# Moving two parts of an S5 operand construction from VectorE to GpSimd

## Chip, cores and metric

The kernel runs on all 8 cores of one Trainium2 chip. Every core has the same program on its own 4096 tokens. The metric is the device time of the slowest core in microseconds.

## What is computed

The reference is one layer of a hybrid encoder: a combined input projection, a gated MLP branch (A), an S5 state space branch (B), a gated merge, and a SwiGLU block. The change touches only constants of branch B. Each of 32 groups has 16 channels and 64 complex states; with the step dt, the recurrence and its readout are

```
mag = exp(lam_re * dt); ab = mag * (cos(lam_im * dt) + i sin(lam_im * dt))
bb  = ((ab - 1) / lam) * b
x_t = ab * x_(t-1) + bb @ u_t
y_t = Re(c @ x_t) + d * u_t
```

The kernel does not scan token by token. It works on blocks of 8 tokens x 16 channels = 128 rows, with matrices made once per group from powers of ab: R_all takes the inputs of a block to its contribution to the state, T_all is the response inside a block, O_all takes the state to the outputs of a block, and D_all (three per group) multiplies the state, real and imaginary parts stacked on 128 partitions, by ab to the 8th, 16th and 24th.

## The kernel before

Each core runs a generation of these matrices, a first main part (eight supertiles of 1024 tokens: norm, projection, block states, a scan over blocks; then the S5 outputs), and a second main part (eight tiles of 512 tokens: the gated MLP, the merge, SwiGLU). The program order of each engine is the order of the calls in the source. A small scheduler in the source holds tokens: `run` makes the engine wait for the tokens of all writers of what is read or written; a `Buf` keeps the tokens of its last writers in `w`.

The generation is `emit_s5_gen`, called once at L302. Its inputs are small loads by SP. Nearly all its arithmetic is on VectorE, with [128, 32] and [128, 32, 16] float32 tiles, through the helper `dv`, which writes the single Buf `G`. So each instruction waits for the one before it, and `G.w` is one token after each `dv`.

- L1089 to L1091 (`wz`) make one slice of 512 columns of a product of complex powers and coefficients, three instructions each. They are called 32 times: 8 positions s, for MR, MRm, Om (float32) and O_all (bf16).
- The group loop makes R_all and T_all for 32 groups: TensorE transposes MR (L1101), ScalarE copies it out (L1103), TensorE multiplies MRm and Om (L1106), VectorE masks the result (L1108) and adds the skip term (L1110). Writers of `G` are kept with `acc=True`, so a group's steps follow each other across the engines.
- Two `cmul` (L1069 to L1074) make the 16th and 24th power. L1119 to L1123 make D_all: for each of 3 powers and 32 groups one tensor_scalar and one fused scalar_tensor_tensor of 128 columns.
- 37 small VectorE instructions (L1004 to L1009, L1129 to L1135) make AA and BB for the scan.

After the generation there is `barrier(skip_pq=True)`: all engines and the SP queue wait for the last token of all engines. Behind it are the load of the projection weights (L324, SP) and the load of the first supertile of x_prev (L336). The latter is issued from the GpSimd queue, as are the conversions of the weights to bf16 in DRAM, of which a first part (L216) is issued ahead of the generation and the rest behind the first x_prev load.

Of the kernel before, what the change touches and what calls it, by code (L numbers as in the profile page):

```python
# [7 lines left out]
F32 = mybir.dt.float32  # L8
BF16 = mybir.dt.bfloat16
AF = mybir.ActivationFunctionType  # L10
ALU = mybir.AluOpType
# [58 lines left out]
def run(E, fns, reads=(), writes=(), acc=False, nowait=False):  # L70
    if not isinstance(fns, (list, tuple)):
        fns = [fns]
    for b in reads:
        for t in b.w:
            E.wait(t)
    for b in writes:
        if nowait:
            continue
        for t in b.w:
            E.wait(t)  # L80
        for t in b.r:
            E.wait(t)
    for f in fns[:-1]:
        E.emit_nosig(f)
    tok = E.emit(fns[-1])
    for b in reads:
        b.r.append(tok)
        if len(b.r) > 64:
            b.r = b.r[-64:]
    for b in writes:  # L90
        if acc:
            b.w.append(tok)
        else:
            b.w = [tok]
            b.r = []
    return tok


def build_program():
# [177 lines left out]
    if S5_ON:  # L277
# [22 lines left out]
        run(SQ, lambda e: e.dma_start(out=S_f, in_=c_swap_f[:, :]), writes=[B_const], acc=True)  # L300
        run(SQ, lambda e: e.dma_start(out=S_bf, in_=c_swap_bf[:, :]), writes=[B_const], acc=True)
        G_gen = emit_s5_gen(run, Buf, dict(PE=PE, ACT=ACT, DVE=DVE, POOL=POOL, SQ=SQ), Alloc(gen_base), dram,  # L302
                            psf, PSF, ident_f, B_const,
                            dict(R_all=R_all, T_all=T_all, O_all=O_all, AA=AA, BB=BB, D_all=D_all, S_f=S_f))
# [609 lines left out]
def emit_s5_gen(run, Buf, E, AL, dram, psf, PSF, ident_f, B_const, outs):  # L914
    PE, ACT, DVE, POOL, SQ = E["PE"], E["ACT"], E["DVE"], E["POOL"], E["SQ"]
    G = Buf()
# [5 lines left out]
    def dv(fn):  # L922
        run(DVE, fn, writes=[G])
# [29 lines left out]
    for i_, dst_ in enumerate((lr2, li2, dcol)):  # L953
        run(PE, lambda e, i_=i_: e.transpose(out=psf[:, 1, 0:32], in_=stg[0:32, i_, :], identity=ident_f[0:32, 0:32]),
            reads=[G, B_const], writes=[PSF[1]])
# [5 lines left out]
    for (cst, C2) in ((cst_re, Cre2), (cst_im, Cim2)):  # L961
        for r in range(4):
            run(PE, lambda e, cst=cst, r=r: e.transpose(out=psf[:, 0, 0:128], in_=cst[:, r, :], identity=ident_f),
                reads=[G, B_const], writes=[PSF[0]])
            run(DVE, lambda e, C2=C2, r=r: e.tensor_copy(out=C2[:, r * 8:(r + 1) * 8, :],
                                                         in_=psf[:, 0, 0:128].rearrange("p (a h) -> p a h", h=16)),
                reads=[PSF[0]], writes=[G])

    def t32():
        return AL.get([32], F32)  # L970
# [63 lines left out]
    Z1 = AL.get([32, 16], F32)  # L1034
    Z2 = AL.get([32, 16], F32)

    def bc16(a):
        return a.unsqueeze(2).to_broadcast([128, 32, 16])
# [7 lines left out]
    lo, hi = slice(0, 64), slice(64, 128)  # L1046
# [8 lines left out]
    Pr = AL.get([16, 32], F32)  # L1055
    Pi_ = AL.get([16, 32], F32)
# [11 lines left out]
    def cmul(orr, oii, xr, xi, yr, yi):  # L1068
        dv(lambda e: e.tensor_tensor(out=t1, in0=xr, in1=yr, op=ALU.mult))  # L1069
        dv(lambda e: e.tensor_tensor(out=t2, in0=xi, in1=yi, op=ALU.mult))  # L1070
        dv(lambda e: e.tensor_tensor(out=orr, in0=t1, in1=t2, op=ALU.subtract))
        dv(lambda e: e.tensor_tensor(out=t1, in0=xr, in1=yi, op=ALU.mult))
        dv(lambda e: e.tensor_tensor(out=t2, in0=xi, in1=yr, op=ALU.mult))
        dv(lambda e: e.tensor_tensor(out=oii, in0=t1, in1=t2, op=ALU.add))  # L1074
# [8 lines left out]
    Om = AL.get([32, 128], F32)  # L1083
    O_all = outs["O_all"]
    tm = AL.get([32, 16], F32)
    tmT = AL.get([128], F32)

    def wz(dst, kidx, A1, A2):
        dv(lambda e: e.tensor_tensor(out=tm, in0=A1, in1=bc16(Pr[:, kidx, :]), op=ALU.mult))  # L1089
        dv(lambda e: e.tensor_tensor(out=dst, in0=A2, in1=bc16(Pi_[:, kidx, :]), op=ALU.mult))  # L1090
        dv(lambda e: e.tensor_tensor(out=dst, in0=dst, in1=tm, op=ALU.add))  # L1091

    for s in range(8):
        wz(MR[:, :, 16 * s:16 * s + 16], 7 + (7 - s), X1, X2)
        wz(MRm[:, :, 16 * s:16 * s + 16], 7 - s, X1, X2)
        wz(Om[:, :, 16 * s:16 * s + 16], 7 + s, Z1, Z2)
        wz(O_all[:, :, 16 * s:16 * s + 16], 7 + s + 1, Z1, Z2)
    R_all, T_all = outs["R_all"], outs["T_all"]
    for g in range(32):
        pb = g % 2  # L1100
        run(PE, lambda e, g=g, pb=pb: e.transpose(out=psf[:, pb, 0:128], in_=MR[:, g, :], identity=ident_f),  # L1101
            reads=[G, B_const], writes=[PSF[pb]])
        run(ACT, lambda e, g=g, pb=pb: e.activation(out=R_all[:, g, :], in_=psf[:, pb, 0:128], func=AF.Copy),  # L1103
            reads=[PSF[pb]], writes=[G], acc=True)
        pt = 2 + g % 2
        run(PE, lambda e, g=g, pt=pt: e.matmul(psf[:, pt, 0:128], MRm[:, g, :], Om[:, g, :], start=True, stop=True),  # L1106
            reads=[G], writes=[PSF[pt]])
        run(DVE, lambda e, g=g, pt=pt: e.tensor_tensor(out=tmT, in0=psf[:, pt, 0:128], in1=maskT, op=ALU.mult),  # L1108
            reads=[PSF[pt], G], writes=[GT_])
        run(DVE, lambda e, g=g: e.scalar_tensor_tensor(out=T_all[:, g, :], in0=ident_f, scalar=dcol[:, g:g + 1], in1=tmT,  # L1110
                                                        op0=ALU.mult, op1=ALU.add),
            reads=[GT_, G, B_const], writes=[G], acc=True)
    D_all, S_f = outs["D_all"], outs["S_f"]
    p16r, p16i, p24r, p24i, c2 = (t32() for _ in range(5))
    cmul(p16r, p16i, Pr[:, 15, :], Pi_[:, 15, :], Pr[:, 15, :], Pi_[:, 15, :])
    cmul(p24r, p24i, p16r, p16i, Pr[:, 15, :], Pi_[:, 15, :])
    tmD = AL.get([128], F32)
    for k, (br_, bi_) in enumerate(((Pr[:, 15, :], Pi_[:, 15, :]), (p16r, p16i), (p24r, p24i))):
        dv(lambda e, bi_=bi_: e.tensor_copy(out=c2[lo], in_=bi_[lo]))  # L1119
        dv(lambda e, bi_=bi_: e.tensor_scalar(out=c2[hi], in0=bi_[hi], scalar1=-1.0, scalar2=None, op0=ALU.mult))  # L1120
        for g in range(32):
            dv(lambda e, g=g: e.tensor_scalar(out=tmD, in0=S_f, scalar1=c2[:, g:g + 1], scalar2=None, op0=ALU.mult))
            dv(lambda e, g=g, k=k, br_=br_: e.scalar_tensor_tensor(out=D_all[:, k, g, :], in0=ident_f, scalar=br_[:, g:g + 1],  # L1123
                                                                    in1=tmD, op0=ALU.mult, op1=ALU.add))
    AA, BB = outs["AA"], outs["BB"]
    for _ in range(5):
        sq_u()
# [5 lines left out]
    dv(lambda e: e.tensor_copy(out=BB[hi, 0:32], in_=A8i[hi]))  # L1133
    dv(lambda e: e.tensor_copy(out=BB[lo, 32:64], in_=A8i[lo]))
    dv(lambda e: e.tensor_scalar(out=BB[hi, 32:64], in0=A8i[hi], scalar1=-1.0, scalar2=None, op0=ALU.mult))  # L1135
    return G


# [46 lines left out]
```

How the kernel before makes its waits and increments, by code:

```python
            def f(eng):  # L889
                for o in E.ops:
                    if o[0] == "w":
                        eng.wait_ge(sems[o[1]], o[2])
                    else:
                        ins = o[1](eng)
                        if o[2] is not None:
                            ins.then_inc(sems[o[2]], o[3])
```

## Time and profile before

| | |
|---|---|
| three runs | 3766.16, 3760.68, 3764.14 us; median 3764.14 us |
| profiled execution | 3765.08 us |
| span of its cores 0 to 7 | 3763.2, 3752.1, 3748.6, 3752.4, 3762.4, 3749.3, 3743.6, 3750.0 us |
| mean granted TensorE clock by core | 0.830 to 0.833 |
| generation (core 0) | from 0 to 440.92 us |

All rows are from core 0, the slowest one. Times are microseconds from the start of the span unless marked ns. "L1122" is the line of the kernel. A group's row gives its total busy time and the mean of one instruction, then the idle time ahead of them on their engine. An arrow names what ended a wait. PE is TensorE, PEld its weight load, DVE VectorE, ACT ScalarE, POOL GpSimd.

### The profile page before, as it was taken

The numbers are of one execution on the slowest core, as the hardware profiler recorded it, in microseconds if no ns is written. First come the engines' busy times: TensorE is split into PE (matmuls) and PEld (weight loads), VectorE is DVE, ScalarE is ACT, GpSimd is POOL, SyncE is SP. The second block draws the span as 40 slices with busy tenths as digits, with TensorE's granted clock in tenths as the row PEclk, the third lists the DMA queues.
The fourth block names the chain that finished last, engine by engine and source line by source line (L and its number), as shares of the span: only waits on it lengthen the run. The fifth ranks groups of instructions, "written<-read, shape, count | busy, mean of one in ns | idle before, by whom it ended". The sixth has DMA issues, their size and how long they took to land.

```text
span 3763.2 us, 43146 instructions; the slowest of 8 cores (3743.6 to 3763.2 us)
## 1 busy us (share of the span) xinstructions
PE 2346.3 (62%) x13686; PEld 1187.1 (32%) x13686; DVE 1249.0 (33%) x3251; ACT 1185.0 (31%) x1714; POOL 89.5 (2%) x168
## 2 busy tenths in 40 slices
PE   0012046666544377957957868777795795796875
PEld 0001024445432133423423423333342342342332
DVE  0753523565633223224213313312322321331321
ACT  0000146655545342242332322323224233232221
POOL 0000001010000000000000000000000000000000
PEclk9999966666666588978978988888897897898988
DMA  2000295897000423423424243243342242433422
GB/s 26 0 0 0 42 109 79 101 124 75 1 7 1 129 79 95 157 89 101 133 97 146 94 137 123 87 143 102 112 143 98 90 146 84 145 99 108 130 87 69
DMA packets 274338, 337.69 MB, mean 90 GB/s; under 512 B 40836, under 2 KB 249640, under 8 KB 273096
## 3 DMA queue, kind: packets, MB, share of 16 engines
q1 hardware_dynamic: 231592, 251.99, 21.4%
q0 software_dynamic: 42528, 82.95, 13.4%
q8 instruction: 118, 1.93, 0.2%
q14 instruction: 100, 0.82, 0.1%
HBM read 367.41 MB, written 49.28 MB: 111 GB/s over the span
## 4 chain that ended last, share of the span: by engine, by line
PE 52%; DVE 17%; ACT 16%; issue 9%; DMA 5%; DVEq 1%; another core or an unknown queue 1%; ACTq 0%; POOLq 0%; POOL 0%; SPq 0%
PE psf L845 8%; PE psf L851 8%; PE psf L860 8%; PE psf L766 5%; PE psf L793 3%; PE psf L812 3%; PE psf L361 3%; PE psf L754 3%; ACT arena L502 2%; DMA out<-arena 2%; DVE arena L671 2%; ACT arena L343 2%; PE psf L799 2%; PE psf L399 1%; PE psf L448 1%
## 5 line engine op out<-in xcount | busy, mean ns | idle before, releaser
L845 PE MATMUL psf<-arena 128*128 128x512 bf16 x1408 | 346.2, 391 | 12.7 <-DVE arena L649 12.7
L851 PE MATMUL psf<-arena 128*128 128x512 bf16 x1408 | 337.3, 383 | 0.0
L860 PE MATMUL psf<-arena 128*128 128x512 bf16 x1408 | 305.2, 379 | 10.1 <-DVE arena L854 10.1
L766 PE MATMUL psf<-arena 128*128 128x512 bf16 x1024 | 254.0, 410 | 83.9 <-ACT arena L769 83.9
L754 PE MATMUL psf<-arena 128*128 128x512 bf16 x512 | 153.7, 468 | 234.0 <-ACT arena L758 234.0
L854 DVE TENSOR_TENSOR arena<-arena,psf 128x512 bf16<-128x512 f32 x176 | 120.8, 687 | 382.9 <-PE psf L851 346.4
L671 DVE TENSOR_TENSOR arena<-arena,psb 128x1024 f32<-128x1024 f32 x64 | 75.9, 1217 | 472.6 <-PE psb L667 472.6
L351 PE MATMUL psb<-arena 128*128 128x128 bf16 x512 | 57.7, 293 | 249.5 <-DMA arena<-x_prev 156.3
L849 ACT ACTIVATE arena<-psf 128x512 f32<-128x512 f32 x176 | 104.2, 597 | 321.2 <-PE psf L845 319.1
L845 PEld LDWEIGHTS psf<-arena 128*128 128x128 bf16 x1408 | 138.5, 100 | 179.9 <-issue 27.9
L851 PEld LDWEIGHTS psf<-arena 128*128 128x128 bf16 x1408 | 139.4, 99 | 172.0 <-issue 10.1
L860 PEld LDWEIGHTS psf<-arena 128*128 128x128 bf16 x1408 | 137.1, 98 | 178.2 <-issue 13.8
L766 PEld LDWEIGHTS psf<-arena 128*128 128x128 bf16 x1024 | 105.0, 104 | 226.8 <-issue 127.3
L793 PE MATMUL psf<-arena 128*128 128x512 bf16 x512 | 134.1, 410 | 45.7 <-DVE arena L746 45.7
L754 PEld LDWEIGHTS psf<-arena 128*128 128x128 bf16 x512 | 58.0, 115 | 327.1 <-issue 292.3
L815 ACT ACTIVATE arena<-psf 128x512 bf16<-128x512 f32 x64 | 38.2, 597 | 319.0 <-PE psf L812 319.0
L1101 PE MATMUL psf<-arena 128*128 128x128 f32 x32 | 14.3, 446 | 193.6 <-DVE arena L1091 154.4
L632 ACT ACTIVATE arena<-arena 128x1024 bf16<-128x1024 f32 x64 | 67.6, 1056 | 208.5 <-DVE arena L631 171.6
L742 DVE TENSOR_TENSOR arena<-arena 128x1024 f32<-128x1024 bf16 x32 | 39.2, 1226 | 278.9 <-ACT arena L736 278.9
L863 ACT ACTIVATE arena<-psf 128x512 bf16<-128x512 f32 x64 | 38.2, 597 | 290.0 <-PE psf L860 290.0
L351 PEld LDWEIGHTS psb<-arena 128*128 128x128 bf16 x512 | 47.1, 133 | 259.0 <-issue 256.7
L812 PE MATMUL psf<-arena 128*128 128x512 bf16 x512 | 115.2, 387 | 15.8 <-DVE arena L805 15.8
(227 smaller groups left out, 3406.8 us busy)
## 6 DMA issues: line engine op xcount, KB each, us to landing
arena<-win_d SPq DMA_DIRECT2D x65, 1024.0 KB, 5.4
arena<-wfd_d SPq DMA_DIRECT2D x64, 704.0 KB, 4.6
arena<-wfg_d SPq DMA_DIRECT2D x40, 1024.0 KB, 5.7
arena<-wfu_d SPq DMA_DIRECT2D x40, 1024.0 KB, 7.8
arena<-x_own POOLq DMA_DIRECT2D x32, 512.0 KB, 6.9
arena<-wa_d SPq DMA_DIRECT2D x16, 1024.0 KB, 10.2
arena<-wo_d SPq DMA_DIRECT2D x16, 1024.0 KB, 6.0
out<-arena POOLq DMA_DIRECT2D x32, 512.0 KB, 2.9
```

The source lines that it names most:

```text
L351: run(PE, [lambda e, k=k, s_=s_, pb=pb, xb_=xb_: e.transpose(out=psb[:, pb, k * 128:(k + 1) * 128], in_=xcm[:, xb_, s_, k * 128:(k + 1) * ...
L361: run(PE, [lambda e, k=k, s_=s_, pb=pb: e.matmul(psf[:, pb, :], hTs[:, k, s_, :], wBg[:, k, :], start=(k == 0), stop=(k == 7)) for k in ra ...
L671: run(DVE, lambda e, b=b, pb=pb, xs=xs: e.tensor_tensor(out=xb2[:, xs, b, :], in0=xb2[:, xs, b, :], in1=psb[:, pb, :], op=ALU.add), reads= ...
L754: run(PE, [lambda e, k=k, gg=gg, pb=pb, wu=wu: e.matmul(psf[:, pb, :], wu[:, k, gg * 128:(gg + 1) * 128], hTa[:, k, :], start=(k == 0), st ...
L766: run(PE, [lambda e, k=k, mm=mm, pb=pb, wg=wg: e.matmul(psf[:, pb, :], wg[:, k, mm * 128:(mm + 1) * 128], hTa[:, k, :], start=(k == 0), st ...
L793: run(PE, [lambda e, k=k, mm=mm, p3=p3, wa_=wa_: e.matmul(psf[:, p3, :], wa_[:, k, mm * 128:(mm + 1) * 128], ya[:, k, :], start=(k == 0), ...
L812: run(PE, [lambda e, k=k, mm=mm, pb=pb, wo_=wo_: e.matmul(psf[:, pb, :], wo_[:, k, mm * 128:(mm + 1) * 128], mg[:, k, :], start=(k == 0), ...
L845: run(PE, [lambda e, k=k, ff=ff, p1=p1, wg_=wg_: e.matmul(psf[:, p1, :], wg_[:, k, ff * 128:(ff + 1) * 128], hTb[:, k, :], start=(k == 0), ...
L849: run(ACT, lambda e, p1=p1, sa=sa: e.activation(out=scr[:, sa, :], in_=psf[:, p1, :], func=AF.Silu), reads=[PSF[p1]], writes=[SCR[sa]])
L851: run(PE, [lambda e, k=k, ff=ff, p2=p2, wu_=wu_: e.matmul(psf[:, p2, :], wu_[:, k, ff * 128:(ff + 1) * 128], hTb[:, k, :], start=(k == 0), ...
L854: run(DVE, lambda e, f=f, p2=p2, sa=sa: e.tensor_tensor(out=act[:, f, :], in0=scr[:, sa, :], in1=psf[:, p2, :], op=ALU.mult), reads=[SCR[s ...
L860: run(PE, [lambda e, f=f, pb=pb, wd_=wd_: e.matmul(psf[:, pb, :], wd_[:, f, :], act[:, f, :], start=(f == 0), stop=(f == NF - 1)) for f in ...
```

## The change

`wz` gets a second form on GpSimd, through a helper `pl` with its own Buf `GP` and its own temporary. Om and O_all use it, in a loop of their own behind the loop for MR and MRm. The product of MRm and Om then also waits for `GP`. D_all goes to GpSimd too; its fused instruction becomes two, since a second tensor_scalar and a tensor_tensor take the place of the scalar_tensor_tensor. The pairs of copies into `c2` are made for all three powers ahead of the D_all loop, into three tiles. At the end the tokens of `GP` are added to those of `G`.

```diff
+    GP = Buf()
+    tmP = AL.get([32, 16], F32)
+
+    def pl(fn):
+        for t_ in G.w:
+            POOL.wait(t_)
+        run(POOL, fn, writes=[GP])
+
+    def wz(dst, kidx, A1, A2, on_pool=False):
+        ex, tt_ = (pl, tmP) if on_pool else (dv, tm)
+        ex(lambda e: e.tensor_tensor(out=tt_, in0=A1, in1=bc16(Pr[:, kidx, :]), op=ALU.mult))
+        ex(lambda e: e.tensor_tensor(out=dst, in0=A2, in1=bc16(Pi_[:, kidx, :]), op=ALU.mult))
+        ex(lambda e: e.tensor_tensor(out=dst, in0=dst, in1=tt_, op=ALU.add))
 
     for s in range(8):
         wz(MR[:, :, 16 * s:16 * s + 16], 7 + (7 - s), X1, X2)
         wz(MRm[:, :, 16 * s:16 * s + 16], 7 - s, X1, X2)
-        wz(Om[:, :, 16 * s:16 * s + 16], 7 + s, Z1, Z2)
-        wz(O_all[:, :, 16 * s:16 * s + 16], 7 + s + 1, Z1, Z2)
+    for s in range(8):
+        wz(Om[:, :, 16 * s:16 * s + 16], 7 + s, Z1, Z2, on_pool=True)
+        wz(O_all[:, :, 16 * s:16 * s + 16], 7 + s + 1, Z1, Z2, on_pool=True)
...
         run(PE, lambda e, g=g, pt=pt: e.matmul(psf[:, pt, 0:128], MRm[:, g, :], Om[:, g, :], start=True, stop=True),
-            reads=[G], writes=[PSF[pt]])
+            reads=[G, GP], writes=[PSF[pt]])
...
-    for k, (br_, bi_) in enumerate(((Pr[:, 15, :], Pi_[:, 15, :]), (p16r, p16i), (p24r, p24i))):
-        dv(lambda e, bi_=bi_: e.tensor_copy(out=c2[lo], in_=bi_[lo]))
-        dv(lambda e, bi_=bi_: e.tensor_scalar(out=c2[hi], in0=bi_[hi], scalar1=-1.0, scalar2=None, op0=ALU.mult))
+    tmD2 = AL.get([128], F32)
+    c2k = [t32() for _ in range(3)]
+    pows = ((Pr[:, 15, :], Pi_[:, 15, :]), (p16r, p16i), (p24r, p24i))
+    for k, (br_, bi_) in enumerate(pows):
+        dv(lambda e, bi_=bi_, k=k: e.tensor_copy(out=c2k[k][lo], in_=bi_[lo]))
+        dv(lambda e, bi_=bi_, k=k: e.tensor_scalar(out=c2k[k][hi], in0=bi_[hi], scalar1=-1.0, scalar2=None, op0=ALU.mult))
+    for k, (br_, bi_) in enumerate(pows):
         for g in range(32):
-            dv(lambda e, g=g: e.tensor_scalar(out=tmD, in0=S_f, scalar1=c2[:, g:g + 1], scalar2=None, op0=ALU.mult))
-            dv(lambda e, g=g, k=k, br_=br_: e.scalar_tensor_tensor(out=D_all[:, k, g, :], in0=ident_f, scalar=br_[:, g:g + 1],
-                                                                    in1=tmD, op0=ALU.mult, op1=ALU.add))
+            pl(lambda e, g=g, k=k: e.tensor_scalar(out=tmD, in0=S_f, scalar1=c2k[k][:, g:g + 1], scalar2=None, op0=ALU.mult))
+            pl(lambda e, g=g, br_=br_: e.tensor_scalar(out=tmD2, in0=ident_f, scalar1=br_[:, g:g + 1], scalar2=None, op0=ALU.mult))
+            pl(lambda e, g=g, k=k: e.tensor_tensor(out=D_all[:, k, g, :], in0=tmD, in1=tmD2, op=ALU.add))
...
+    G.w = list(G.w) + list(GP.w)
     return G
```

## Rows read from the trace of the kernel before

**Rows 1.** The page: busy time by engine; the span in 40 slices.
```profile
PE 2346.3 (62%) x13686; PEld 1187.1 (32%) x13686; DVE 1249.0 (33%) x3251; ACT 1185.0 (31%) x1714; POOL 89.5 (2%) x168
PE   0012046666544377957957868777795795796875
DVE  0753523565633223224213313312322321331321
ACT  0000146655545342242332322323224233232221
DMA  2000295897000423423424243243342242433422
```

**Rows 2.** Windows: stretch, its length, busy us and instructions by engine, clock, DMA.
```profile
160.90:238.10 77.20, 0.00 (x0) 0.00 (x0) 66.45 (x96) 0.00 (x0) 0.00 (x0) 1.00 0.00 0
238.10:341.90 103.80, 38.82 (x96) 21.86 (x96) 20.55 (x64) 10.15 (x33) 0.00 (x0) 1.00 0.00 0
341.90:346.30 4.40, 0.00 (x0) 0.00 (x0) 2.66 (x14) 0.00 (x0) 0.00 (x0) 1.00 0.01 2
346.30:430.15 83.85, 0.00 (x0) 0.00 (x0) 61.96 (x196) 0.00 (x0) 0.00 (x0) 1.00 0.00 0
430.15:441.00 10.85, 0.00 (x0) 0.00 (x0) 6.96 (x37) 0.00 (x0) 0.00 (x0) 1.00 0.00 0
```

**Rows 3.** The chain that ended last, behind the barrier.
```profile
442.93 22.18 DMA arena<-x_prev
465.25 1.16 ACT arena L343 x2
```

**Rows 4.** Groups of VectorE, the first of the `wz` lines; all three alike.
```profile
L1089 DVE TENSOR_TENSOR arena<-arena 128x512 f32<-128x512 f32 x32 | 22.2, 692 | 3.7 <-DVE arena L1091 0.5
```

**Rows 5.** Timeline: first and last `wz` instruction, first instructions of the group loop.
```profile
160.98 0.69 DVE L1089 TENSOR_TENSOR arena<-arena 128x512 f32<-128x512 f32 x1
...
237.31 0.69 DVE L1091 TENSOR_TENSOR arena<-arena 128x512 bf16<-128x512 bf16 x1
...
238.25 0.45 PE L1101 MATMUL psf<-arena 128*128 128x128 f32 x1 [154.44 <-DVE arena L1091]
238.84 1.28 ACT L1103 ACT_TABLE_LOAD   x1 [238.84 <-PE psf L1101]
...
240.56 0.77 PE L1106 MATMUL psf<-arena 128*128 128x128 f32 x2 [1.86 <-ACT arena L1103]
```

**Rows 6.** Timeline: end of the group loop, `cmul`, start of D_all.
```profile
341.48 0.35 DVE L1110 SCALAR_TENSOR_TENSOR arena<-arena 128x128 bf16<-128x128 f32 x1
341.93 0.19 DVE L1069 TENSOR_TENSOR arena<-arena 128x32 f32<-128x32 f32 x1
...
345.84 0.17 DVE L1119 COPY arena<-arena 64x32 f32<-64x32 f32 x1
346.12 0.18 DVE L1120 TENSOR_SCALAR arena<-arena 64x32 f32<-64x32 f32 x1
346.40 0.28 DVE L1122 TENSOR_SCALAR arena<-arena 128x128 f32<-128x128 f32 x1
```

**Rows 7.** Groups of VectorE from 341.9 to 442.
```profile
L1123 DVE SCALAR_TENSOR_TENSOR arena<-arena 128x128 bf16<-128x128 f32 x96 | 33.8, 352 | 11.1 <-DVE arena L1122 1.4
L1122 DVE TENSOR_SCALAR arena<-arena 128x128 f32<-128x128 f32 x96 | 27.5, 286 | 10.3
```

**Rows 8.** Timeline: last instruction of the generation, first DMA behind the barrier.
```profile
440.74 0.18 DVE L1135 TENSOR_SCALAR arena<-arena 64x32 f32<-64x32 f32 x1
...
442.93 0.55 POOL L336 DMA_DIRECT2D arena<-x_prev  x1 [368.50 <-issue]
```

**Rows 9.** GpSimd: timeline of two dependent memsets; two groups of the whole span.
```profile
74.11 0.10 POOL L958 MEMSET arena<- 128x1 f32 x1 [54.53 <-DMA arena<-c_mask_toep]
74.33 0.10 POOL L959 MEMSET arena<- 128x1 f32 x1
...
L677 POOL DMA_DIRECT2D arena<-x_own x32 | 16.9, 530 | 1.5 <-issue 0.3
L589 POOL MEMSET arena<- 128x128 bf16 x1 | 0.2, 204 | 398.8 <-DVE arena L587 398.8
```

More of the change, by code:

```diff
@@ L1086, in emit_s5_gen @@
     tmT = AL.get([128], F32)
[L1088 to L1091, printed above, removed]
+    GP = Buf()
[9 more added lines that the diff above has]
+        ex(lambda e: e.tensor_tensor(out=dst, in0=dst, in1=tt_, op=ALU.add))
     for s in range(8):
@@ L1113, in emit_s5_gen @@
     D_all, S_f = outs["D_all"], outs["S_f"]
-    p16r, p16i, p24r, p24i, c2 = (t32() for _ in range(5))
+    p16r, p16i, p24r, p24i = (t32() for _ in range(4))
     cmul(p16r, p16i, Pr[:, 15, :], Pi_[:, 15, :], Pr[:, 15, :], Pi_[:, 15, :])
```

## The prediction

> **What bounds the kernel now.** I read the page first, for where the changed code sits, then the windows by stage, then the timeline at each seam, then the groups of the two engines concerned. The page shows [rows 1]: TensorE is the busiest engine at 62% of the span, VectorE has 33%, GpSimd 2%. Taken as averages they say that VectorE is not the bound and that GpSimd has room. The slices say something else about the changed code: it lies in the first 441 us, where TensorE and ScalarE are nearly idle, the DMA share is 0 after the first 60 us, and VectorE is the only busy engine. The windows cut that stretch up [rows 2]: the four products MR, MRm, Om and O_all (96 VectorE instructions in 77 us, nothing else running), the loop over 32 groups (T_all and R_all, TensorE 38.8 us, VectorE 20.6 us and ScalarE 10.2 us of 103.8 us, one after another), 4.4 us of powers, the D_all loop (196 instructions in 83.9 us, again VectorE alone), and 37 small instructions in 10.9 us. Then comes the barrier, and behind it the first load of x_prev starts the main work: the chain of waits goes from the end of this stretch into that DMA and from it into ScalarE [rows 3]. So every microsecond by which the last operand is finished later or earlier moves all 3320 us behind it by the same amount. Nothing in this prologue is covered by anything else. That the engine shares call GpSimd free is beside the point; what counts is whether GpSimd works at the same time as VectorE, and how long its chain is.
>
> **Can the two engines overlap?** The new helper copies G.w at the time of the call, and each call on VectorE has replaced G.w by its own last token. The Om and O_all calls are written after all MR and MRm calls, so the first GpSimd product waits for the last MRm add. The D_all calls are written after the group loop, after the two cmul and after the six c2k copies, so they wait for the last of these. While GpSimd makes Om and O_all, VectorE has nothing: its next instruction is the mask multiply of group 0 (L1108), which needs TensorE's MRm x Om product, and that now waits for GP, the last token of all 48 GpSimd instructions, O_all's included. TensorE runs in order, so behind that wait are queued the transposes of groups 1 to 31; ScalarE waits for those, VectorE for the products. Only the transpose of group 0 and ScalarE's table load get ahead. The one real overlap is D_all on GpSimd beside the last 37 VectorE instructions.
>
> **The change part by part**, on the profiled execution's time base:
>
> 1. MR and MRm stay on VectorE. The four products run from 160.98 to 238.00 [rows 4, 5]: 77.0 us for 96 instructions, 0.80 us each (692 ns busy and a gap of 0.1 us). Half of them end at 161.0 + 38.5 = 199.5.
> 2. Om and O_all: 48 GpSimd instructions of 512 columns, at p each from start to start. A wait across engines costs 0.25 us, as from the last add to TensorE's transpose (238.00 to 238.25) [rows 5]. They run from 199.75 to 199.75 + 48p.
> 3. The group loop, from TensorE's first MRm x Om at 240.56 to the end of the last L1110 at 341.83, is 101.3 us [rows 5, 6]. The table load of 1.28 us that stood ahead of that matmul is now hidden under item 2. End of loop: 199.75 + 0.25 + 48p + 101.3 = 301.3 + 48p.
> 4. Twelve cmul instructions (341.93 to 345.84, 3.9 us) and now all six c2k halves at 0.28 us (1.7 us) instead of two [rows 6]: 5.6 us, and 0.25 us to reach GpSimd. D_all starts at 307.1 + 48p.
> 5. D_all: VectorE needed 96 pairs of 286 and 352 ns [rows 7]. GpSimd needs 96 triples (two tensor_scalar and one tensor_tensor of 128 columns, because the fused operation is split), t each, and every one waits for the one before, since all write GP. End: 307.1 + 48p + 96t.
> 6. The 37 small VectorE instructions (10.9 us) leave the path; they end at about 307 + 11 + 48p, under item 5. If GpSimd were so fast as to finish inside them they would set the end again.
> 7. Now the end is at 440.92 [rows 8], and from there to the x_prev issue it is 2.0 us, which stays: the same waits, on the same GpSimd queue, ahead of the same DMA. No DMA is moved past anything; the 10 early conversions on that queue have been issued long before, and the later ones stand behind the barrier before and after. SP's queue waits at the same barrier.
>
> So the change is 48p + 96t - 133.8 us. The break-even is 133.8 us of GpSimd work in 336 instructions, 0.40 us each.
>
> **What is p, what is t?** The trace has no GpSimd arithmetic at all, only memsets and DMA issues [rows 9]. Two dependent memsets of one column start 0.22 us apart; a memset of 128 columns takes 204 ns against 98 ns, so a column costs 0.835 ns in one pass that only writes. Bounds from these rows:
> - Below: every instruction costs one pass, whatever it reads. p = 0.22 + 0.43 = 0.65, t = 3 x 0.327 = 0.98; 31 + 94 = 125 us, a gain of 8.5 us. An instruction can't be cheaper than a memset of its size.
> - Inputs are read one after the other and the write is hidden behind: p = 0.22 + 0.855 = 1.075, t = 0.327 + 0.327 + 0.434 = 1.09; 52 + 104 = 156 us, a loss of 22 us.
> - Every operand, read or written, costs its pass: p = 0.22 + 1.28 = 1.50, t = 0.434 + 0.434 + 0.541 = 1.41; 72.1 + 135.2 = 207 us, a loss of 73.5 us.
> - Above: the fixed part is not a memset's 0.22 us but that of the other GpSimd instruction of the trace, a DMA issue with 0.53 us. That adds 0.31 x 336 = 104 us: a loss of 178 us.
> I take the third. The memset is the nearest row for the fixed part, but it reads nothing, and the new instructions also fetch a pointer scalar, a broadcast operand or a strided output; so I count all passes instead of hiding one. It would make an Om instruction (about 1.4 us busy) twice as long as VectorE's 692 ns. The weight of a fixed part above 0.22 us is on the high side of the range: each 0.1 us there is 34 us.
>
> The Trainium skill, "GPSIMD Engine Reference", section "Performance versus the Vector engine", speaks against the change: a two-input elementwise instruction costs about 2.6 cycles of 1.2 GHz per element there, one with a single input about line rate, and VectorE is roughly twice as fast. No row here shows GpSimd arithmetic to hold that against. Worked out from the page as an estimate, p = 1.33 and t = 1.15, together 174 us, a loss of 40 us instead of 73.5.
>
> **Sum**: 207.3 - 133.8 = +73.5 us. The profiled execution took 3765.1 us (span 3763.2 us), 0.9 us above the median of 3764.1. On the median: 3837.6 us, 2.0% slower.
>
> **Rivals.**
> - *Passes overlap.* Cheaper reads, 22 to 45 us of loss, 3786 to 3809 us. For it: a streaming engine need not serialize its write. Against it: only a write-only row gives the slope. 0.17.
> - *Fixed cost dominates.* 288 of the 336 instructions have only 128 columns, so if dispatch plus the wait for one's own predecessor is 0.35 to 0.53 us, the loss is 117 to 178 us, 3881 to 3942 us. For it: the DMA issues at 0.53 us each. Against it: the two dependent memsets at 0.22 us. 0.18.
> - *The other side: one pass for every operation.* If GpSimd takes p = 0.65 and t = 0.98, the end comes at 432 and the kernel takes about 3756 us, 0.2% faster, because the 10.9 us of small VectorE instructions and the table load are hidden. It decides where 336 GpSimd instructions average under 0.40 us. For it only the write-only slope; against it, no row shows this engine reading a tensor at that rate. 0.04.
> - *Contention.* The 37 VectorE instructions beside D_all could hold GpSimd up, at most by their own busy time, 7 us; 3845 us. The change as written would be hurt little, because it overlaps so little. 0.03.
> - *The split loop does not do what it says.* If Om really ran beside MR, 38.5 us would be saved and the loss would be 35 us. The token list excludes it: G.w holds the last MRm add when the first GpSimd product is written. 0.00.
>
> The rule on contention is in the Trainium skill, "SBUF — State Buffer", section "SBUF: two separate sides": VectorE with two SBUF inputs and a GpSimd instruction that reads SBUF hold a shared port pair exclusively, one fully blocking the other. By it the contention rival is real, for some 7 us.
>
> TensorE's clock stays out of the sum. The granted clock is 1.00 (2.4 GHz) over the whole stretch [rows 2], though TensorE had been idle for 154 us before the group loop; a longer wait ahead of it should leave it there.
>
> **How the numbers follow.** My forecast has 0.58: 3815 to 3860 us, p and t within some 10% of the third case. With the others: the range from 3790 to 3915 us takes in the upper half of the overlapping case and the dispatch case up to a fixed part of 0.45 us; some 0.07 is left out below it and 0.08 above. What this kernel's measurement can tell from no change is some 0.2% (7.5 us), so faster 0.03, same 0.03, slower 0.94.
>
> **What the changed profile would show.** VectorE empty from about 199.5 until the first L1108; 48 GpSimd instructions there with 1.5 us from start to start; TensorE's first MRm x Om at about 272; a group loop of the same 101 us; D_all on GpSimd from about 379 to 514, with triples of 1.4 us; VectorE done at about 390 and idle after; the x_prev issue at about 516 instead of 442.93. Everything after it the same, shifted. The prediction is wrong if triples take under 1.0 or over 2.0 us, or if the main part, from the x_prev issue to the end, changes its length.

## The result and the profile after

The changed kernel takes 3901.12 us (median of 9 runs) against 3765.76 us for the kernel before (median of 10 runs): a ratio of 1.0357, 95% interval 1.0344 to 1.0369, so 3.6% and some 135 us slower. Executions in which one die of the chip was disturbed occur with every kernel here; the ratios leave them out, and where too few others are left below, the profiled execution is given instead.

The page of the kernel after (its slowest core is core 7) answers to [rows 1]:

```profile
PE 2348.0 (60%) x13686; PEld 1188.7 (31%) x13686; DVE 1155.1 (30%) x3011; ACT 1185.0 (30%) x1714; POOL 302.2 (8%) x504
DVE  1712001456563322322322312322321331331321
POOL 0051770101000000000000000000000000000000
```

VectorE has lost 94 us of work and GpSimd has gained 213 us. A slice is 97 us long here, and only in the third and the fourth do both have a digit. The windows by stage show that even there they hardly work at the same time; the columns are those of [rows 2], the busy time of PE, PEld, DVE, ACT and POOL in this order, then the clock and the DMA:

```profile
160.00:198.86 38.86, 0.00 (x0) 0.00 (x0) 33.42 (x49) 0.00 (x0) 0.00 (x0) 1.00 0.00 0
198.86:259.00 60.14, 0.48 (x2) 0.25 (x2) 0.00 (x0) 1.56 (x2) 53.08 (x48) 1.00 0.00 0
259.00:360.50 101.50, 38.34 (x95) 21.60 (x95) 20.34 (x64) 8.59 (x31) 0.00 (x0) 1.00 0.00 0
360.50:366.50 6.00, 0.00 (x0) 0.00 (x0) 3.92 (x21) 0.00 (x0) 0.00 (x0) 1.00 0.00 0
366.50:575.50 209.00, 0.00 (x0) 0.00 (x0) 7.28 (x36) 0.00 (x0) 159.39 (x288) 1.00 0.00 0
```

The first two rows are the first row of [rows 2] torn in two: VectorE for 39 us, then GpSimd for 60 us with VectorE at zero. The group loop takes what it took before, 101.5 us (before, 101.3 us from TensorE's first MRm x Om on). D_all has 209 us instead of 84 us. The seams in the timeline of core 7 answer to [rows 5, 6, 8]:

```profile
199.01 1.05 POOL L1098 TENSOR_TENSOR arena<-arena 128x512 f32<-128x512 f32 x1 [125.17 <-DVE arena L1100]
...
257.66 1.16 POOL L1100 TENSOR_TENSOR arena<-arena 128x512 bf16<-128x512 bf16 x1
...
258.96 0.77 PE L1116 MATMUL psf<-arena 128*128 128x128 f32 x2 [59.41 <-POOL arena L1100]
...
360.36 0.35 DVE L1120 SCALAR_TENSOR_TENSOR arena<-arena 128x128 bf16<-128x128 f32 x1
...
368.13 0.66 POOL L1136 TENSOR_SCALAR arena<-arena 128x128 f32<-128x128 f32 x1 [109.32 <-issue]
...
574.97 0.45 POOL L1138 TENSOR_TENSOR arena<-arena 128x128 bf16<-128x128 f32 x1
577.38 0.63 POOL L336 DMA_DIRECT2D arena<-x_prev  x1 [1.96 <-issue]
```

TensorE waited 59.4 us for the last O_all instruction, whose result it doesn't read. The x_prev issue comes at 577.38 instead of 442.93; averaged over the eight cores it is 576.6 against 442.3, 134.3 us later, which is the whole loss (the medians differ by 135.4 us). From that issue to the end it is 3317.1 us (core 7), against 3320.3 us before (core 0). The groups of GpSimd hold what [rows 9] could not show:

```profile
L1136 POOL TENSOR_SCALAR arena<-arena 128x128 f32<-128x128 f32 x96 | 58.0, 604 | 125.9 <-issue 109.3 <-POOL arena L1138 16.5
L1137 POOL TENSOR_SCALAR arena<-arena 128x128 f32<-128x128 f32 x96 | 58.0, 604 | 16.5 <-POOL arena L1136 16.5
L1138 POOL TENSOR_TENSOR arena<-arena 128x128 bf16<-128x128 f32 x96 | 43.5, 453 | 14.9 <-POOL arena L1137 0.9
L1098 POOL TENSOR_TENSOR arena<-arena 128x512 f32<-128x512 f32 x16 | 16.9, 1056 | 127.3 <-DVE arena L1100 125.2
```

A tensor_scalar, which reads one tensor, is dearer than a tensor_tensor of the same size, 604 against 453 ns. VectorE needs 286 ns for it [rows 7].

### The profile page after: what moved, and what is told of

Read it like the earlier page. It is cut to its first block, busy times and chain, and to the rows that moved or that the text cites. A ratio compares the mean times of both kernels' runs of the same rounds, so it can differ in the third digit from the quotient of the medians.

```text
span 3894.5 us, 43373 instructions; the slowest of 8 cores (3879.3 to 3894.5 us)
## 1 busy us (share of the span) xinstructions
PE 2348.0 (60%) x13686; PEld 1188.7 (31%) x13686; DVE 1155.1 (30%) x3011; ACT 1185.0 (30%) x1714; POOL 302.2 (8%) x504
## 4 chain that ended last, share of the span: by engine, by line
PE 50%; ACT 15%; DVE 13%; issue 9%; POOL 6%; DMA 5%; another core or an unknown queue 1%; DVEq 1%; ACTq 0%; POOLq 0%; SPq 0%
PE psf L845 8%; PE psf L860 8%; PE psf L851 8%; PE psf L766 5%; PE psf L793 3%; PE psf L812 3%; PE psf L361 3%; PE psf L754 3%; ACT arena L502 2%; DMA out<-arena 2%; DVE arena L671 2%; ACT arena L343 2%; PE psf L799 2%; POOL arena L1137 2%; POOL arena L1136 2%
## 5 line engine op out<-in xcount | busy, mean ns | idle before, releaser
L879 POOL DMA_DIRECT2D out<-arena x32 | 17.1, 533 | 2422.3 <-DVE arena L869 2371.8
L793 PE MATMUL psf<-arena 128*128 128x512 bf16 x512 | 133.9, 409 | 45.2 <-DVE arena L746 45.2
L632 ACT ACTIVATE arena<-arena 128x1024 bf16<-128x1024 f32 x64 | 67.6, 1056 | 210.6 <-DVE arena L631 171.5
```

Source lines behind the costliest of these rows:

```text
L793: run(PE, [lambda e, k=k, mm=mm, p3=p3, wa_=wa_: e.matmul(psf[:, p3, :], wa_[:, k, mm * 128:(mm + 1) * 128], ya[:, k, :], start=(k == 0), ...
```

## The experiments

In what follows "the issue" is the time of the first x_prev issue, the mean of the eight cores; it is where the prologue ends. The kernel before has it at 442.3, the changed kernel at 576.6. The stretch behind it lasts 3306 to 3326 us (mean of the cores) in every profiled execution below, whatever was moved in the prologue, so the issue says more sharply than the time of a run what an edit did.

The issue has a drift of its own. All kernels have the same code up to L1040, the first VectorE instruction of 512 columns, and yet they don't reach it at the same time; on core 0 of the kernel before and on core 7 of the changed one:

```profile
122.31 0.69 DVE L1040 TENSOR_TENSOR arena<-arena 128x512 f32<-128x512 f32 x1
...
121.70 0.69 DVE L1040 TENSOR_TENSOR arena<-arena 128x512 f32<-128x512 f32 x1
```

The mean of the cores is 121.6 in the kernel before, 120.9 in the changed kernel and 118.6 to 119.8 in the experiments; why is not known. So the issue is also given counted from L1040 (mean of the cores, us):

| kernel | issue | from L1040 to the issue | against the kernel before |
|---|---|---|---|
| before | 442.3 | 320.7 | |
| after | 576.6 | 455.7 | +135.0 |
| e1_products_only | 459.4 | 339.8 | +19.1 |
| e2_dall_only | 555.2 | 435.5 | +114.8 |
| e3_forms | 559.9 | 440.8 | +120.1 |
| e9_less_waiting | 536.4 | 417.8 | +97.1 |
| e4_overlap | 435.2 | 315.7 | -5.0 |
| e4b_overlap_again | 435.1 | 315.7 | -5.0 |
| e5_batch_pool | 443.2 | 324.1 | +3.5 |
| e6_batch_vector | 398.4 | 278.8 | -41.9 |
| e7_overlap_batch | 393.1 | 274.0 | -46.7 |
| e8_vector_pipelined | 317.7 | 198.3 | -122.4 |
| e10_pipelined_overlap | 313.0 | 194.0 | -126.7 |

In the code cuts, `...` stands for what is left out.

**One part alone, e1_products_only.** D_all is back on VectorE:

```diff
-            pl(lambda e, g=g, k=k: e.tensor_scalar(out=tmD, ...))
-            pl(lambda e, g=g, br_=br_: e.tensor_scalar(out=tmD2, ...))
-            pl(lambda e, g=g, k=k: e.tensor_tensor(out=D_all[:, k, g, :], in0=tmD, in1=tmD2, op=ALU.add))
+            dv(lambda e, g=g, k=k: e.tensor_scalar(out=tmD, ...))
+            dv(lambda e, g=g, k=k, br_=br_: e.scalar_tensor_tensor(out=D_all[:, k, g, :], ...))
```

> Only Om and O_all are on GpSimd, D_all is back on VectorE. Theory A (the two parts add, each is its GpSimd chain less the VectorE chain that it replaces): 48 x 1.25 us of GpSimd less 38.5 us of VectorE less 2 us for the hidden table load, +20 us, some 3785 us, and the part behind the x_prev issue keeps its 3317 to 3320 us. Theory B (waking GpSimd inside the prologue costs something of its own, or what follows gets slower): more than +30 us here, and the two parts together make more than the 135 us of the whole change.

Measured: a ratio to the kernel before of 1.0042 (95% interval 1.0027 to 1.0058, as for the ratios below), +16 us; the issue is at 459.4, +17.1 us, or +19.1 us counted from L1040. Theory A had +20.

**The other part alone, e2_dall_only.** The four products are in one loop on VectorE again, D_all stays on GpSimd.

> Only D_all is on GpSimd, the four products are on VectorE. Theory A: 96 triples of 2.16 us less 96 pairs of 0.87 us, plus 1 us for the copies, less the 10.9 us that are now beside it: some +115 us, 3880 us; with the other part it makes the whole 135 us. If fixed cost by instruction dominates (the rival 'fixed cost' of the prediction), this part, which has 288 of 336 instructions, has over 80% of the loss. Theory B: the sum of both parts differs from the whole by more than 10 us.

Measured: 1.0293 (1.0260 to 1.0325), +110 us; the issue is at 555.2, +112.9 us, or +114.8 us counted from L1040, where theory A had +115. Counted from there the two parts make 133.9 us of the 135.0 us of the whole, D_all having 86% of them. The part behind the issue lasts 3306 to 3310 us (mean of the cores) with all four kernels. Theory A stands: two chains, added up, with 1 us left over.

**What is dear in a GpSimd tensor_scalar, e3_forms.** A first instruction of another form for each power:

```diff
-            pl(lambda e, g=g, k=k: e.tensor_scalar(out=tmD, in0=S_f, scalar1=c2k[k][:, g:g + 1], ...))
+            if k == 0:
+                pl(lambda e: e.tensor_scalar(out=tmD, in0=S_f, scalar1=0.5, ...))
+            elif k == 1:
+                pl(lambda e, g=g: e.tensor_scalar(out=tmD[:, 0:64], in0=S_f[:, 0:64], scalar1=c2k[1][:, g:g + 1], ...))
+            else:
+                pl(lambda e, g=g: e.tensor_tensor(out=tmD, in0=S_f, in1=c2k[2][:, g:g + 1].to_broadcast([128, 128]), ...))
```

> As the changed kernel, but the first of the three GpSimd instructions of D_all has another form for each power (this changes D_all for the first two powers): for the first an immediate instead of a pointer scalar, for the second 64 columns instead of 128, for the third a tensor_tensor with the scalar broadcast along the row. In the changed kernel it takes 604 ns and is 0.77 us from the next. Theory A (fetching the pointer scalar is what makes it dearer than the 453 ns of the tensor_tensor): the immediate form falls to 0.35 us or less, the broadcast form takes 0.45 us. Theory B (tensor_scalar is a slow routine on this engine whatever its scalar): the immediate form keeps some 0.60 us, the broadcast form takes 0.45 us. The 64 column form gives the split: 0.50 us if a column costs what it costs in a tensor_tensor (1.57 ns, from 453 ns at 128 and 1056 ns at 512), 0.55 us if it costs a memset's 0.835 ns.

The groups of GpSimd in this run; L1137 has the immediate, L1139 the 64 columns, L1142 the broadcast:

```profile
L1144 POOL TENSOR_SCALAR arena<-arena 128x128 f32<-128x128 f32 x96 | 57.9, 603 | 16.7 <-POOL arena L1142 5.8 <-POOL arena L1137 5.6 <-POOL arena L1139 5.3
L1137 POOL TENSOR_SCALAR arena<-arena 128x128 f32<-128x128 f32 x32 | 17.1, 535 | 114.5 <-issue 109.3 <-POOL arena L1145 5.1
L1139 POOL TENSOR_SCALAR arena<-arena 128x64 f32<-128x64 f32 x32 | 14.1, 442 | 5.8 <-POOL arena L1145 5.8
L1142 POOL TENSOR_TENSOR arena<-arena 128x128 f32<-128x128 f32 x32 | 12.7, 398 | 4.6
```

The pointer is worth 68 ns of the 603, so theory A falls and B stands, though not wholly (0.60 was expected and 0.54 came). The 64 column form is off both numbers that I had given: (603 - 442) / 64 is 2.5 ns a column, dearer than the 1.57 ns of a tensor_tensor that reads twice as much. Two widths give no more than an estimate of that slope. Writing the same product as a tensor_tensor with a broadcast operand saves a third, 398 ns. Why a tensor_scalar is so slow here stays open.

**How much of a gap is the wait, e9_less_waiting.** `tmD` and `tmD2` are doubled, with Bufs of their own, so that only the tensor_tensor waits for a near predecessor:

```diff
-            pl(lambda e, g=g, k=k: e.tensor_scalar(out=tmD, ...))
+            run(POOL, lambda e, g=g, k=k, i=i: e.tensor_scalar(out=tmD[:, i], ...), writes=[B1[i]])
```

> As the changed kernel, but the temporaries of D_all are doubled and have Bufs of their own, so that neither tensor_scalar waits for the instruction just ahead of it; only the tensor_tensor waits for its two inputs. Theory A (the gaps of 0.14 to 0.17 us between instructions are the round trip of the token): the two gaps ahead of the tensor_scalars go, a triple falls from 2.14 to some 1.8 us, 32 us in all: some 3868 us. Rival (the gap is the engine's own change from one instruction to the next, with or without a wait): triples stay at 2.1 us, 3900 us.

The timeline on GpSimd:

```profile
470.04 0.60 POOL L1141 TENSOR_SCALAR arena<-arena 128x128 f32<-128x128 f32 x1
470.61 0.60 POOL L1142 TENSOR_SCALAR arena<-arena 128x128 f32<-128x128 f32 x1
471.36 0.45 POOL L1143 TENSOR_TENSOR arena<-arena 128x128 bf16<-128x128 f32 x1
471.80 0.60 POOL L1141 TENSOR_SCALAR arena<-arena 128x128 f32<-128x128 f32 x1
```

A triple (two tensor_scalar and one tensor_tensor) takes 1.76 us instead of 2.14, and the issue comes at 536.4, 40 us before that of the changed kernel, or 38 us counted from L1040. Theory A, a little over its 32 us: without the wait the next instruction even starts before the end of the one ahead (470.61, where the one ahead ends at 470.64). The ratio, 1.0299 (1.0179 to 1.0419), is too wide to add anything.

**Can the engines overlap, e4_overlap.** As e1_products_only, with the order of two loops turned round, so that the tokens that GpSimd waits for end at the powers:

```diff
-    for s in range(8):
-        wz(MR[:, :, 16 * s:16 * s + 16], 7 + (7 - s), X1, X2)
-        wz(MRm[:, :, 16 * s:16 * s + 16], 7 - s, X1, X2)
     for s in range(8):
         wz(Om[:, :, 16 * s:16 * s + 16], 7 + s, Z1, Z2, on_pool=True)
         wz(O_all[:, :, 16 * s:16 * s + 16], 7 + s + 1, Z1, Z2, on_pool=True)
+    for s in range(8):
+        wz(MR[:, :, 16 * s:16 * s + 16], 7 + (7 - s), X1, X2)
+        wz(MRm[:, :, 16 * s:16 * s + 16], 7 - s, X1, X2)
```

> As e1_products_only, but the GpSimd products are written ahead of the loop for MR and MRm, so that they wait for the powers alone and run beside VectorE. Theory A (the loss of this part is the missing overlap): 60 us of GpSimd cover the 38.5 us of VectorE, the first product of TensorE starts at about 222 instead of 240.6, and the time is 38.5 us under that of e1_products_only: 3746 us, 19 us under the kernel before. Rival (the two engines exclude each other on a port, the products have two inputs in SBUF on both): VectorE's 48 instructions and GpSimd's 48 take turns, their stretch is 60 + 38 = 98 us and the time is that of e1_products_only, 3785 us.

The timeline where both engines work:

```profile
161.09 1.51 POOL L1100 TENSOR_TENSOR arena<-arena 128x512 f32<-128x512 f32 x1
161.60 1.55 DVE L1098 TENSOR_TENSOR arena<-arena 128x512 f32<-128x512 f32 x1
162.75 1.32 POOL L1098 TENSOR_TENSOR arena<-arena 128x512 f32<-128x512 f32 x1
163.26 1.36 DVE L1099 TENSOR_TENSOR arena<-arena 128x512 f32<-128x512 f32 x1
164.21 1.32 POOL L1099 TENSOR_TENSOR arena<-arena 128x512 bf16<-128x512 f32 x1
164.72 1.36 DVE L1100 TENSOR_TENSOR arena<-arena 128x512 f32<-128x512 f32 x1
165.68 1.42 POOL L1100 TENSOR_TENSOR arena<-arena 128x512 bf16<-128x512 bf16 x1
166.18 1.47 DVE L1098 TENSOR_TENSOR arena<-arena 128x512 f32<-128x512 f32 x1
```

VectorE's 692 ns have become 1360 ns, GpSimd's 1056 have become 1320, and they alternate: one instruction of each every 1.5 us (4.58 us for three, from 161.60 to 166.18). Each ends behind the other engine's: VectorE's at 164.62 is 0.55 us behind the end of GpSimd's at 164.07, and that one is 0.92 us behind the end of VectorE's at 163.15. That is neither the free overlap (1.25 us, GpSimd's pitch) nor the sum of both pitches (0.80 + 1.25 = 2.05 us). The issue is at 435.2, 7.1 us before the kernel before (5.0 us counted from L1040) and 24 us better than e1_products_only, where theory A had 38.5 and the rival 0. Both were wrong in size: the engines exclude each other for a part of each instruction. I ran it again as e4b_overlap_again:

> The kernel of e4_overlap once more, for a ratio with an interval. By its profile the x_prev issue comes 7 us earlier than in the kernel before (mean of the cores 435.2 against 442.3), so 3757 us where the kernel before has 3764. Theory A: 0.998, within 0.2% of no change or just beyond. Rival (full overlap): 0.995.

The issue came at 435.1 and the profiled execution took 3756.68 us, the first one 3756.44. Neither has a ratio with an interval, so the gain against the kernel before stays a reading of the profile.

**Few long instructions, on GpSimd: e5_batch_pool.** These 9 instructions stand in place of the 288 of the changed kernel; `tmD` and `tmD2` have 32 x 128 columns:

```diff
     for k, (br_, bi_) in enumerate(pows):
+        pl(lambda e, k=k: e.tensor_tensor(out=tmD, in0=S_f.unsqueeze(1).to_broadcast([128, 32, 128]),
+                                          in1=c2k[k].unsqueeze(2).to_broadcast([128, 32, 128]), op=ALU.mult))
+        pl(lambda e, br_=br_: e.tensor_tensor(out=tmD2, in0=ident_f.unsqueeze(1).to_broadcast([128, 32, 128]),
+                                              in1=br_.unsqueeze(2).to_broadcast([128, 32, 128]), op=ALU.mult))
+        pl(lambda e, k=k: e.tensor_tensor(out=D_all[:, k], in0=tmD, in1=tmD2, op=ALU.add))
```

> The changed kernel with D_all still on GpSimd behind the group loop, but as 9 tensor_tensor instructions of 4096 columns (32 groups at once, scalars and the two 128 column matrices broadcast) instead of 288 small ones. Theory A (the loss was the number of instructions and the dear form, not the elements): with 1.57 ns a column and 0.25 us fixed, 9 x 6.7 = 60 us in place of 208, so 148 us under the changed kernel: 3753 us, 12 us under the kernel before. Rival (columns read through a broadcast or written over long rows are dearer, 2.17 ns or more): 80 us or more, 3773 us.

Measured: 0.9991 (0.9954 to 1.0028), the issue at 443.2. Each product takes 7.03 us, each add 8.80 us (6.7 was expected), 69 us in all instead of 207, between theory A's 60 and the rival's 80. So 133 of the 134 us go away (131.6 of 135.0 counted from L1040) with the D_all work still on GpSimd and still behind the group loop.

The long instructions bring a new price with them. From the timeline of core 4, with VectorE's last 37 small instructions beside D_all:

```profile
365.20 7.03 POOL L1135 TENSOR_TENSOR arena<-arena 128x4096 f32<-128x4096 f32 x1 [109.29 <-issue]
365.24 7.05 DVE L1005 TENSOR_TENSOR arena<-arena 128x32 f32<-128x32 f32 x1
372.38 7.03 POOL L1137 TENSOR_TENSOR arena<-arena 128x4096 f32<-128x4096 f32 x1
372.38 7.07 DVE L1006 TENSOR_TENSOR arena<-arena 128x32 f32<-128x32 f32 x1
379.55 8.80 POOL L1139 TENSOR_TENSOR arena<-arena 128x4096 bf16<-128x4096 f32 x1
379.56 8.83 DVE L1007 TENSOR_SCALAR arena<-arena 128x32 f32<-128x32 f32 x1
...
426.18 8.86 POOL L1139 TENSOR_TENSOR arena<-arena 128x4096 bf16<-128x4096 f32 x1
...
440.42 0.18 DVE L1150 TENSOR_SCALAR arena<-arena 64x32 f32<-64x32 f32 x1
```

Instructions of 0.2 us take 7 to 9 us: each of the nine GpSimd instructions holds one of VectorE's until it has ended, on every core, and L1007, which has a single tensor input, is held like the others. So 19 of the 37 are still to do when GpSimd ends (435.04), and the chain ends on VectorE, 5.6 us later.

**The same on VectorE, e6_batch_vector.** The kernel before with these 9 instructions through `dv`.

> The kernel before with D_all on VectorE as the same 9 batched instructions. Theory A: VectorE's 512 columns take 692 ns, 128 take 286 to 352, so a column is 1.04 ns: 4096 are 4.4 us, 9 are 40 us in place of 83 us: 3722 us, 43 us under the kernel before with nothing moved to another engine. Rival (VectorE is slowed by broadcast rows or by the float32 temporaries of 16 KB a partition): little or no gain, 3755 us or more.

Measured: 0.9852 (0.9781 to 0.9924); the issue at 398.4, 44 us earlier, or 42 us counted from L1040. An instruction takes 4.42 us, theory A's 4.4:

```profile
L1136 DVE TENSOR_TENSOR arena<-arena 128x4096 f32<-128x4096 f32 x3 | 13.3, 4425 | 0.3
```

**Full overlap as the change meant it, e7_overlap_batch.** Powers first; GpSimd makes Om, O_all and D_all in 9 instructions; the group loop waits for Om alone.

> What the change was meant to be: powers first, then GpSimd makes Om, O_all and the batched D_all while VectorE makes MR and MRm and goes through the group loop, which waits for Om alone. Theory A (the engines share a port only for the time of their reads, as in e4_overlap, where 48 instructions on each took 72 us): MR ends at about 238, the group loop is unchanged, D_all is done under it, the end comes at 351 instead of 441: 3675 us. Rival (a GpSimd instruction holds VectorE off for its whole read, 5 us and more where it has 4096 columns): each of the 9 long instructions stops VectorE's two-input steps of the group loop, the loop grows by 40 to 60 us: 3715 to 3735 us.

Measured: 0.9841 (0.9782 to 0.9900), the issue at 393.1, 49 us earlier (47 us counted from L1040), where theory A had 90. The timeline in the group loop:

```profile
261.25 7.03 POOL L1120 TENSOR_TENSOR arena<-arena 128x4096 f32<-128x4096 f32 x1
...
263.70 0.29 DVE L1138 TENSOR_TENSOR arena<-psf,arena 128x128 f32<-128x128 f32 x1 [2.44 <-PE psf L1136]
264.09 4.33 DVE L1140 SCALAR_TENSOR_TENSOR arena<-arena 128x128 bf16<-128x128 f32 x1
268.42 7.03 POOL L1122 TENSOR_TENSOR arena<-arena 128x4096 f32<-128x4096 f32 x1
```

L1138 has one input in PSUM and takes its old 0.29 us with GpSimd busy beside it. L1140 has both inputs in SBUF, takes 4.33 us instead of 0.35 and ends when the GpSimd instruction has ended. Over the loop its 32 instructions have 51.8 us instead of 32 times the 0.35 us of [rows 6]: the loop grows by 41 us. The rival was right. The interval doesn't tell this kernel from e6_batch_vector, which has nothing on GpSimd; at the issue it is 5 us better. This is the case of the Trainium skill, "SBUF — State Buffer", section "SBUF: two separate sides" (an exclusive lock for the whole instruction when VectorE has two SBUF inputs and GpSimd reads SBUF), and the trace agrees, 4.33 us, up to the end of a 7.03 us instruction.

**Everything on VectorE, e8_vector_pipelined.** e6_batch_vector with the group loop untied:

```diff
+    G0, GR, GTA = Buf(), Buf(), Buf()
+    G0.w = list(G.w)
+    tmTs = AL.get([2, 128], F32)
+    GTs = [Buf(), Buf()]
...
-            reads=[PSF[pb]], writes=[G], acc=True)
+            reads=[PSF[pb]], writes=[GR])
...
-            reads=[G, GP], writes=[PSF[pt]])
+            reads=[G0], writes=[PSF[pt]])
...
-            reads=[GT_, G, B_const], writes=[G], acc=True)
+            reads=[GTs[pb], G0, B_const], writes=[GTA])
+    G.w = list(G.w) + list(GR.w) + list(GTA.w)
```

The three pairs are R_all on ScalarE, MRm x Om on TensorE and T_all on VectorE.

> As e6_batch_vector, all on VectorE, and the group loop gets a Buf for each product and two temporaries, so that group g+1 does not wait for group g on all engines. Theory A (the loop is a chain of latencies, 3.19 us a group, with 1.2 us of TensorE and 0.85 us of VectorE in it): it falls to 1.3 to 1.5 us a group, from 102 to about 46 us, on top of the 43 us of the batch: 3665 us. Rival (the PSUM buffers or TensorE's float32 passes bound it near 2.5 us): 3700 us.

Measured: 0.9658 (0.9584 to 0.9731), median 3655 us where the kernel before had 3780 us beside it, the issue at 317.7, 125 us earlier (122 us counted from L1040). A group takes 0.66 us instead of 3.19, faster than either number that I gave. The 1.2 us of TensorE in a group, of which the expectation made its bound, was no bound: in the old loop the records of TensorE's instructions are longer. The matmul pair of L1106 took 0.77 us in [rows 5], here

```profile
251.65 0.46 PE L1119 MATMUL psf<-arena 128*128 128x128 f32 x2
251.71 0.28 ACT L1116 ACTIVATE arena<-psf 128x128 bf16<-128x128 f32 x1 [0.38 <-PE psf L1114]
251.87 0.28 DVE L1121 TENSOR_TENSOR arena<-psf,arena 128x128 f32<-128x128 f32 x1
```

**And GpSimd added to that, e10_pipelined_overlap.** e8 with Om and O_all on GpSimd, written first.

> As e8_vector_pipelined, but Om and O_all are made on GpSimd beside MR and MRm on VectorE. Theory A (where both engines run two-input instructions from SBUF they take turns for their reads, 1.465 us for one of each, as in e4_overlap): 48 of each take 71 us instead of VectorE's 77 us alone, 6 us better than e8_vector_pipelined, no more, although half of the work has left VectorE. Rival (in e4_overlap something else held VectorE): the stretch is 60 us, 17 us better.

The issue comes at 313.0, 4.7 us before e8 (4.3 us counted from L1040): theory A (the two engines need 72.9 us for the products, from 158.58 to 231.47 on core 5, where VectorE alone had 77.0). The ratio is 0.9649 (0.9495 to 0.9803), too wide to tell the two apart; the profiled execution took 3641.52 us. Read from the profile, half of the product work off VectorE is worth 4 to 5 us.

## Why the prediction was right, and where its size came from

The direction, the place and the mechanism were right: two chains on GpSimd, nothing hidden behind VectorE, all later work shifted by the same amount. The size was not. Forecast were +73.5 us, measured are +134.3 us at the issue. The measured 3901.12 us lie in the stated range of 3790 to 3915 us, but not in the 3815 to 3860 us of the forecast itself, which had 0.58; they lie where the rival *fixed cost dominates* stood with 0.18. One of the prediction's own signs of being wrong came true: a triple of D_all takes 2.14 us, over its limit of 2.0. That the range held the result it owes to having been widened for that rival, not to the sum. Step by step, the times of core 7 against those forecast for core 0:

1. MR and MRm on VectorE end at 198.85 in place of 199.5. Right.
2. No overlap of the products: VectorE has 0.00 us from 198.86 to 259. Right. 48p was put at 72.1 us and is 59.8 (199.01 to 258.82, p = 1.25), -12.3 us. "Every operand costs its pass" was too dear for these instructions.
3. The group loop: 101.3 forecast, 101.75 found (258.96 to 360.71). The table load is hidden. Right.
4. From its end to the first GpSimd instruction of D_all: 5.85 forecast, 7.4 found. The 1.6 us stand between the end of VectorE's last copy (365.94) and GpSimd's start (368.13). Ahead of that instruction stand the waits for TensorE's 32 reads of `GP`; the first GpSimd product, which has none of these, starts 0.16 us behind VectorE's last add (198.85 to 199.01). That the waits are the 1.6 us is argued only.
5. D_all: the term that was mis-sized. 96t was put at 135.2 us and is 207.3 (368.13 to 575.42, t = 2.16 for 1.41): +72.1 us. A tensor_scalar was put at 0.434 us from start to start and takes 0.75 to 0.77, the tensor_tensor was put at 0.541 and takes 0.60 to 0.62.
6. and 7. The 37 small instructions lie beside D_all, the barrier takes its 2.0 us, the rest is unchanged. Right. (The early DMAs on GpSimd's queue are eight conversions and two small loads, not ten conversions; nothing rests on that.)

The forecast had the issue at 516.4 on core 0. With -0.65 (item 1), -0.2 (two hand-overs between engines that took 0.16 and 0.14 us instead of 0.25), -12.3, +0.5, +1.6 and +72.1 it comes to 577.4, where it is.

**The step that failed** is the price of a small GpSimd instruction, above all its fixed part, which the prediction took from two memsets at 0.22 us from start to start. An estimate of what it is: a tensor_scalar of 128 columns is busy for 604 ns, of which 128 columns at the 2.5 ns of e3_forms are 320 and 280 are fixed; with the gap of 0.15 to 0.17 us behind it, 0.44 us are fixed. A tensor_tensor has 453 - 128 x 1.57 = 250 ns and the gap, 0.42 us. That is 0.2 us and more above 0.22 in each of the 288 instructions, some 61 us of the 72. The tensor_scalar's dear columns (0.32 us where two passes of 0.107 were counted) add 21 us, and the tensor_tensor's cheap ones (0.20 us where three passes were counted) take off 12 us. Part of the fixed part is the wait for the predecessor's token: without two of the three waits e9_less_waiting has 38 to 40 us less. The prediction's slope also came from a poor row: the memset of 128 columns in [rows 9] writes bf16, not float32.

The rivals: *fixed cost dominates* (117 to 178 us) gave the better number, and its condition, 0.35 to 0.53 us for dispatch and the wait for one's own predecessor, is met by the estimate, 0.42 to 0.44 us. It kept the third case's columns, though, which are too dear for the tensor_tensor and too cheap for the tensor_scalar; the size of its number is in part luck. *Passes overlap* holds for the columns of the tensor_tensor alone (1.57 ns, where three passes are 2.5). *The other side*, 0.40 us for an average instruction, is out: the 336 average 0.79 us. *Contention* was real as a mechanism and nearly absent in the change as made, for want of overlap: the GpSimd instructions beside VectorE's last 37 took up to 0.66 us instead of 0.60, under 1 us in all. It eats the gain of a better version (e4, e7) and sets the end of e5. The estimate from the Trainium skill, "GPSIMD Engine Reference", sections "Performance versus the Vector engine" and "Engine selection", had p = 1.33, nearer to 1.25 than mine, and t = 1.15, further from 2.16 than mine; its line rate for a single input is not what the trace shows, 2.5 ns a column and 604 ns.

## What to carry to other kernels

Before an engine's idle share is taken for room, look at whether the stage that would be moved is a chain: here the prologue was one, and moving links of it to a slower engine without moving their waits lengthened it by the difference. In such a chain the number of instructions and what each waits for are worth more than the engine: nine instructions instead of 192 gave 42 to 44 us, and a Buf for each product 81 us more, both on the engines that had the work. Where the price of an engine is not in the trace, one small instruction of the kind to be moved, timed from start to start, is worth more than any row of another kind. Work on GpSimd beside work on VectorE between SBUF tiles was worth little here, since the engines take turns; what might go there is work whose counterpart on VectorE reads PSUM. No run tried a kernel of that kind.

## What was not expected of the hardware

- On GpSimd the time from the start of one small instruction to that of the next, which waits for it, has a fixed part of 0.42 to 0.44 us (estimated from 64, 128 and 512 columns), where two memsets suggested 0.22 us.
- On GpSimd a tensor_scalar costs more than a tensor_tensor: float32, 128 columns, 604 ns with a pointer scalar, 535 ns with an immediate, against 398 ns for a tensor_tensor with the scalar broadcast (453 ns for the one that writes bf16 from two tiles).
- With 512 columns on both engines, VectorE and GpSimd settle into strict alternation, 1.5 us for a pair, where they need 0.80 and 1.25 us alone.
- A VectorE instruction with both inputs in SBUF waited for the end of a long GpSimd instruction (4.33 us, once 6.12 us in e7; 7.05 to 8.84 us for instructions of 0.19 us in e5). So did a tensor_scalar with a single tensor input in SBUF (8.83 us in e5). One with an input in PSUM did not wait at all (0.29 us in e7).
